# Normalisation factors applied behind the input projections of a four-layer hybrid block

## The reference, cut to what matters

```
def hybrid_layer(x, norm_g, w_in, w_out, ...):              # first kind, twice
    h = rmsnorm(x, norm_g)                                  # x * rsqrt(mean(x*x)+1e-6) * g
    proj = einsum("bsd,de->bse", h, w_in)                   # 14 pieces of 256 columns
    y_a = silu(layernorm(conv31(a_u*sigmoid(a_v)) + b)) * silu(a_z)
    y_b = b_b * conv3(b_c * b_x) * silu(b_z)
    y_c = window_gqa(...) * silu(c_z)      # keys at most 128 positions away
    y_d = neighborhood_attn(...) * silu(d_z)
    return x + concat(y_a, y_b, y_c, y_d) @ w_out

x = rmsnorm(x, final_norm_g)                                # between the two kinds

for l in range(2):                                          # second kind
    h = rms_norm(x, g_mix[l]);  proj = h @ w_in[l]
    # pool mixer; causal attention with rms_norm(q_lat, g_q), rms_norm(c_kv, g_kv);
    # a linear recurrence; gates = sigmoid(gate_logit + b_gate)
    x = x + (gates[0]*y_pool + gates[1]*y_mla + gates[2]*y_lru) @ w_out[l]
    h = rms_norm(x, g_ffn[l])
    x = x + square(relu(h @ w_ff1[l])) @ w_ff2[l]
return rms_norm(x, g_final)
```

## Time and profile before

| | |
|---|---|
| median of 3 runs | 2291.18 us (2290.15 to 2292.41) |
| the profiled execution: its time, its span | 2291.51 us, 2289.3 us |
| PE busy | 2085.9 us, 91% |
| weight loads of PE busy | 1728.9 us, 76% |
| DVE busy | 1306.3 us, 57% |
| ACT busy | 756.3 us, 33% |
| POOL busy | 1067.6 us, 47% |
| mean granted clock of PE | 0.945 of full speed |

### The profile page before, as it was taken

How to read it: one execution, slowest core, us unless ns; L and a number is a source line. 1 busy time by engine, 2 the same in 40 slices (tenths; PEclk the granted TensorE clock), 3 DMA queues, 4 the chain that set the end, 5 groups by cost and what they waited for, 6 DMA issues and landing times.

```text
span 2289.3 us, 30906 instructions
## 1 busy us (share of the span) xinstructions
PE 2085.9 (91%) x9708; PEld 1728.9 (76%) x9708; DVE 1306.3 (57%) x2241; ACT 756.3 (33%) x1101; POOL 1067.6 (47%) x1301
## 2 busy tenths in 40 slices
PE   5988887998887899979999999978899899999997
PEld 4877666877665788868788888867787788888886
DVE  5377766378768655464545535465555445535445
ACT  3232332332332344443232232234444323232231
POOL 3333244334233343456656655634435465656653
PEclk9999898999897899989999999989989899999998
DMA  4111112212111121122222222211222222222221
GB/s 153 64 57 71 38 56 80 76 55 74 38 56 67 56 74 55 74 92 85 89 100 95 92 92 96 106 63 57 73 73 74 77 107 79 106 92 92 96 98 62
DMA packets 28052, 179.66 MB, mean 78 GB/s; under 512 B 4000, under 2 KB 4128, under 8 KB 7456
## 3 DMA queue, kind: packets, MB, share of 16 engines
q1 hardware_dynamic: 24192, 169.88, 20.7%
q10 hardware_dynamic: 3744, 8.34, 1.1%
HBM read 176.11 MB, written 2.10 MB: 78 GB/s over the span
## 4 chain that ended last, share of the span: by engine, by line
issue 48%; POOL 35%; PE 17%; DVE 0%; POOLq 0%; DVEq 0%; ACT 0%
POOL W_lo L422 35%; PE bank L436 16%; POOLq L417 0%; DVE X L1626 0%; PE bank L486 0%; PE bank L479 0%; POOLq L419 0%; POOL spare L413 0%; DVE TMP L1283 0%; DVE PR L1328 0%; DVE PRE L1325 0%; DVE X L1989 0%; DVE PR L1986 0%; DVEq L182 0%; POOLq L422 0%
## 5 line engine op out<-in xcount | busy, mean ns | idle before, releaser
L422 POOL TENSOR_TENSOR W_lo<-W_raw,W_hi 128x256 fp32r<-128x256 f32 x1280 | 1065.7, 868 | 1189.7 <-ACT W_hi L867 1189.6
L436 PE MATMUL bank<-H_hi,W_hi 128*128 128x512 f32 x1392 | 560.3, 402 | 20.2 <-POOL W_lo L422 17.4
L436 PE MATMUL bank<-H_lo,W_hi 128*128 128x512 f32 x1392 | 549.8, 395 | 0.0
L436 PE MATMUL bank<-H_hi,W_lo 128*128 128x512 f32 x1392 | 549.7, 395 | 0.0
L867 ACT ACTIVATE W_hi<-W_raw 128x2048 fp32r<-128x2048 f32 x161 | 307.4, 1910 | 395.3 <-PE bank L436 382.5
L436 PE MATMUL bank<-Y_hi,W_hi 128*128 128x512 f32 x836 | 338.3, 405 | 21.9 <-DVE Y_lo L1268 11.8
L436 PE MATMUL bank<-Y_lo,W_hi 128*128 128x512 f32 x836 | 335.5, 401 | 0.0
L436 PE MATMUL bank<-Y_hi,W_lo 128*128 128x512 f32 x836 | 335.1, 401 | 0.0
L436 PEld LDWEIGHTS bank<-H_hi,W_hi 128*128 128x128 f32 x1392 | 267.4, 192 | 82.3 <-issue 22.3
L436 PEld LDWEIGHTS bank<-H_hi,W_lo 128*128 128x128 f32 x1392 | 265.9, 191 | 57.6
L436 PEld LDWEIGHTS bank<-H_lo,W_hi 128*128 128x128 f32 x1392 | 267.1, 192 | 53.0
(11 more groups left out here) (265 smaller groups left out, 2753.2 us busy)
## 6 DMA issues: line engine op xcount, KB each, us to landing
W_raw<-in_stream SPq DMA_DIRECT2D x160, 1024.0 KB, 4.8
BT<-in_bias ACTq DMA_DIRECT2D x8, 448.0 KB, 3.6
X<-in_x ACTq DMA_DIRECT2D x4, 512.0 KB, 9.7
out<-X SPq DMA_DIRECT2D x8, 256.0 KB, 2.2
BT<-in_rope ACTq DMA_DIRECT2D x2, 512.0 KB, 3.5
MC<-in_causal ACTq DMA_DIRECT2D x2, 320.0 KB, 3.0
MS<-in_window ACTq DMA_DIRECT2D x1, 320.0 KB, 11.0
CS<-in_rope ACTq DMA_DIRECT2D x1, 256.0 KB, 2.5
```

The lines of the kernel that those rows point to most:

```text
L422: ins = nc.gpsimd.tensor_tensor(W[1][:, s, part], W_raw[:, s, part], W[0][:, s, part].bitcast(F32), ALU.subtract)
L436: mm = pe.matmul(out, lhs[a], rhs[b], start=(not begun and k == 0 and a == 0 and b == 0), stop=(not more and k == n - 1 and a == 1), skip_ ...
```

## The change

Three things change.

1. The factor of a token, r = 1/sqrt(mean(x²)+eps), is the same for all features, so (X·r·g)W = ((X·g)W)·r. H is now the split of X·g, not of the normalised value. ACT makes H_hi from X with the gain as scale, DVE makes H_lo in one instruction (`norm_lo`), both for tile k as soon as output tile k of the layer before is added to X. PE starts the next layer's first unit at once and computes the sums of squares between its tiles 5 and 6. The factor, spread over partitions, is copied to SBUF (RB1, RB2), and each chunk's result is multiplied with it on DVE. For the second kind's first layer the norm between the kinds is folded in as well: a second sum (ACCG), with the squared gains, gives both factors, and X itself is normalised later (`norm_between`).
2. Blocks of 128 keys that the mask leaves out altogether are no longer computed (`b1_reach`, `b2_reach`): in the window attention two or three blocks a row of queries, not three; in the causal attention 1, 2, 3, 4 blocks, not 2, 2, 4, 4.
3. The hardware loops over the two layers of each kind are written out (`for l in range(DEPTH)`); the inner loops stay. The sums of squares in the feed-forward part are left out but for the last round.

The core of the diff:

```
+        def norm_lo(b, l, k, gain):
+            dve.wait_ge(b.hi.sem, b.hi.at(l, f"n{k}"))
+            nc.vector.scalar_tensor_tensor(H[1][:, k, :], X[:, k, :], gain, H[0][:, k, :].bitcast(F32),
+                                           ALU.mult, ALU.subtract).then_inc(...)
-            norm_to_h(b1, l, "n", "n", PAR1[:, P1["norm_g"]:P1["norm_g"] + KT])
+            mean(b1, l, "n")
+            diagonals(b1, l, "n")
+            nc.vector.tensor_copy(RB1[:, :], NB[:, :]).then_inc(dve_step, own.step())
...
+            def scaled(name, out, bank_):
+                nc.vector.tensor_tensor(out, bank_[:, :], RB1[:, :], ALU.mult) \
+                    .then_inc(b1.free.sem, own.event(b1.free, l, name))
+            def rescaled(out):
+                dve.wait_ge(*own.last(0))
+                nc.vector.tensor_tensor(out, out, RB1[:, :], ALU.mult).then_inc(dve_step, own.step())
...
                 elif kind in ("bz", "az"):                      # DVE
-                    dve.wait_ge(b1.aux.sem, b1.aux.at(l, name))
-                    nc.vector.scalar_tensor_tensor(pre, TH, 1.0, bank_[:, :], ALU.add, ALU.mult) \
-                        .then_inc(b1.free.sem, own.event(b1.free, l, name))
+                    scaled(name, pre, bank_)
+                    dve.wait_ge(b1.aux.sem, b1.aux.at(l, name))
+                    nc.vector.scalar_tensor_tensor(pre, TH, 1.0, pre, ALU.add, ALU.mult)
...
                 elif kind in ("dz", "cz", "bz", "az"):          # ACT
-                    nc.scalar.activation(TH, bank_[:, :], ACT.Tanh, scale=0.5)
+                    act.wait_ge(b1.free.sem, b1.free.at(l, name))
+                    nc.scalar.activation(TH, of, ACT.Tanh, scale=0.5)
...
+            for mm in by_tiles(pe, 0, H, lambda kt: pe.wait_ge(b1.lo.sem, b1.lo.at(l, f"n{kt}")),
+                               {6: lambda: pe_sums(pe, b1, l, "n", (ACC1,))} if l else {}):
                 mm.then_inc(b1.done.sem, 1)
+            if not l:
+                pe_sums(pe, b1, l, "n", (ACC1,))
+            chunk("dk0")
+            pe_spread(pe, b1, l, "n")
...
+    def b1_reach(i):
+        return ((0, 4), (0, 4)) if i < STEPS else (((0, 2), (0, 3)), ((0, 3), (1, 3)))[i % 2]
+    def b2_reach(s):
+        return (((0, 1), (0, 2)), ((0, 3), (0, 4)))[s % 2]
...
+                    def gate(s):                                # DVE, heads of the second kind
+                        dve.wait_ge(b2.done.sem, b2.done.at(l, f"g{jj}{s}", "h", j))
+                        nc.vector.tensor_tensor(out, G[c][:, :], RB2[:, :], ALU.mult) \
+                            .then_inc(b2.free.sem, own.event(b2.free, l, f"g{jj}{s}", "h", j))
```

More of the change, by code:

```diff
@@ L60 @@
 NP2 = _n
+GAINS = {"b1": (0, KT), "b2": (2 * KT, 3 * KT), "between": 4 * KT, "last": 5 * KT}
 COUNTS = []
@@ L929, in begin, with values @@
                     prep(1, l, k, (b1.done, l, B1_CHUNKS[2 * k - 3]))
+            def values(name, col):
+                act.wait_ge(b1.done.sem, b1.done.at(l, "ck1" if name == "cv" else name))
+                for t in range(4):
+                    act.wait_ge(*own.last(1))
+                    ins = nc.scalar.activation(AV[0][:, t, col:col + P], G[col // P if name[0] == "d" else 1]
+                                               [:, t * P:(t + 1) * P], ACT.Copy, scale=NR[:, t:t + 1])
+                    if t == 3:
+                        ins.then_inc(b1.hi.sem, own.event(b1.hi, l, name))
+                    else:
+                        ins.then_inc(act_step, own.step())
             def chunk(name, begun=False):
@@ L1644, in _ @@
+            diagonals(b2, l, "n", spread=False)
+            if not l:
+                dve.wait_ge(*own.last(1))
+                nc.vector.reciprocal(NR[:, 4:8], NR[:, 4:8]).then_inc(dve_step, own.step())
+                diagonal(bf, 0, "between", TMP[:, 1, :], 4)
             dve.wait_ge(par_in, 32 * l + 96)
             dve.wait_ge(*own.last(1))
-            nc.vector.tensor_scalar(HB[:, 0:4], PAR2[:, P2["b_a"]:P2["b_a"] + 4], 0.5, None, ALU.mult) \
+            nc.vector.tensor_scalar(HB[:, 0:28], HB[:, 0:28], 0.5, None, ALU.mult) \
@@ L1663, in _ @@
             mark(b2.acc, l, "kv")
+            dve.wait_ge(b2.bc.sem, b2.bc.at(l, "n"))
+            dve.wait_ge(*own.last(1))
+            nc.vector.tensor_copy(RB2[:, :], OB[:, :]).then_inc(dve_step, own.step())
             lam = PAR2[:, P2["lam"]:P2["lam"] + 2]
@@ L1712, in q_latent @@
                     mark(b2.acc, l, "q")
-            dve.wait_ge(b2.ss.sem, b2.ss.at(l, "kv"))
+            mean(b2, l, "kv", 2 * P, EPA[:, :])
             q_latent(0)
-            diagonals(b2, l, "kv")
+            diagonals(b2, l, "kv", spread=False)
+            if not l:
+                dve.wait_ge(bf.bc.sem, bf.bc.at(0, "between"))
+                norm_between(range(4))
+            dve.wait_ge(b2.bc.sem, b2.bc.at(l, "kv"))
             for k in (3, 4):
@@ L1723, in _ @@
             q_latent(1)
+            if not l:
+                norm_between(range(4, KT))
             q_latent(2)
@@ L2003, in _ @@
             own.leave(3)
[L2004 to L2009 removed]
+            down("f3", 0, True)
+        mean(bf, 0, "n")
+        diagonals(bf, 0, "n")
+        final_norm()
 def tables():
```

590 lines of the change are left out of this document (351 added, 239 removed).

## The result

The changed kernel took 2303.26 us in the median of four runs (2302.4 to 2305.71); the kernel before, run beside it, took 2290.66 us. The ratio is 1.0055 with a 95% interval of 1.0039 to 1.0071: it is slower by half a per cent. The forecast was 2264.7, in a range up to 2280, with a chance of 0.05 for slower.

A forecast was written before the change was run, and what follows sets the result against it. PE was taken to bound the whole, with DVE bounding the second kind's starts and the first kind's attention stage. Border gains less added DVE work summed to −26.8 us, from 2291.5 to 2264.7 us; range 2249 to 2280.

The forecast's parts named there:

- Rival 2: At the borders W_lo takes the norm's place: two units per border, 1 us each, some 6 us, so 2271; 15%.
- Rival 3: Attention stage, first kind: thirteen instructions and six DVE-ACT hand-overs cost 25.8 us a layer, so 2296, slower; 5%.
- start up to dk0, with the spread: Program start: dk0 begins at 37.0 not 43.48 us; less 1.05 for the spread between dk0 and dk1, −5.4.
- border in the first kind, with the spread: First kind, layer 1 to 2: PE's gap from o31 to dk0 shrinks from 31.4 to 13.0 us; with spread −17.4.
- first to second kind: Border between the kinds: PE's gap from o31 to q00 shrinks from 37.2 to 15.0 us, −22.1.
- starts of the second kind, both: DVE bounds these starts; later LS, the kr multiplication, the mean and norm_between add 8.2 us in the first layer, 5.0 in the second.
- first scores to first output unit, both layers: First kind's attention stage: DVE's additions in line, less shorter key-block rows, plus POOL contention: +10.2 us a layer, +20.4 in all.
- causal heads, both layers: Left-out key blocks save transposes and score products, 0.74 us per head pair, −5.9 over eight; gate multiplications cost nothing.
- middle and end of the second kind: Third gate's tanh waits for a DVE multiplication, 0.95 us a layer, +1.9; last norm's mean on DVE, +0.3.
- the trips: First kind's attention: DVE to ACT to DVE hand-overs in cz, bz and az, 7.7 us a layer.
- the multiplications behind au, bx and bb: First kind's attention: six a layer on DVE, only bx0, bb0 and bb1 in line, 2.2 us a layer.
- The term for LS: Starts of the second kind: DVE's little chain LS stands behind the copy of RB2, so begins 3.9 us later.

The follow-up runs named there:

- e1_early: The changed kernel with ACT rounding the values' W_hi ahead of AQ_hi of dq0, not behind AQ_hi of dq1; 2243.33 us, ratio 0.9785.
- e5_ls: As e1_early, with the chain LS ahead of the copy of RB2 on DVE in the second kind's start; 2241.06 us, ratio 0.9782.
- e9_best: e1_early with LS moved up, step 8's maxima between cz0's multiplication and gate, and W_hi ahead of H_hi in output units and last feed-forward round; 2234.88 us.
- e3_late8: The kernel before the change, with only the values' W_hi made once dk1 is projected, not once dq1 is; 2349.28 us, ratio 1.0249.

## Why the prediction was wrong, point by point

The step that failed is the sentence in the paragraph on the attention stage of the first kind: "From the projections' end to 137.80 PE has no pause, and DVE is busy 37.70 of 94.30, so the dq, dk, dv and dz multiplications cost nothing; that cover would be gone only with 50 us more of DVE." I measured the cover by DVE's busy time. What mattered was what stood behind the readers of dq in the list of another engine. A chunk's AQ_hi on ACT now waits for the factor, and the W_hi of the unit after next waits behind AQ_hi, while PE reaches that unit 7.8 us earlier than before. The sum moved dk0 forward and took for granted that the weights would follow. The runs showed in place of "cost nothing" a pause of 7.3 us and 19.7 us of low clock in each layer, 54 us in all. Before, AQ_hi read the bank, H had the factor in it already, and dk0 (at 390.82 in the earlier trace rows) was followed by the values without a pause. I listed the multiplication of dq and its cost, yet did not name what was queued behind the instruction that waits for it. Rival 2 had the right mechanism (W_lo takes the norm's place) but placed it at the by-tiles unit, at 1 us each, and without the clock; "the prepared units are two ahead" was wrong in just this place. Rival 3, the one on the slower side, named another mechanism and was not it.

Both parts are in the trace, and e1_early undid both: the pause, and the low clock in the values (41.2 us for 21.5). They are 54 of the 60 us that e1_early gave back; the rest lies in the first 5 us behind the values, which still had the low clock, and in the spread of the executions.

The other terms of the sum, the changed kernel against the profile before:

| term | forecast | measured |
|---|---|---|
| start up to dk0, with the spread | −5.4 | −7.8 |
| border in the first kind, with the spread | −17.4 | −17.7 |
| first to second kind | −22.1 | −22.3 |
| border in the second kind | −11.8 | −12.6 |
| starts of the second kind, both | +13.2 | +6.0 |
| first scores to first output unit, both layers | +20.4 | +17.8 |
| causal heads, both layers | −5.9 | −11.3 |
| output units of the first kind | 0 | +4.7 |
| middle and end of the second kind | +2.2 | about 0 |
| dk1 to the first scores, both layers | 0 | +53.9 |

Without the last row the sum is −43, and e1_early measured −48.6 with its own medians (2243.33 against 2291.98). So the chance of 0.92 for faster stood on terms that were mostly right or too cautious, and on one that was missing. The other terms didn't add up to the forecast either: they had −26.8 and measured −43, and e1_early, which has no missing term, is 21 us below the 2264.7 and below the 2249 of the range. The sum would have missed on that side too.

- The borders were right to within 1 us. The by-tiles unit took the 10.9 us at full clock that the earlier trace rows gave. The start of the program was 2.4 us better than forecast, and its arithmetic was wrong as well: 4.5 tiles at 3.4 us from 13.0 on and the rest at 2.2 end at about 36, not 34. The last H_lo was there at 32.3.
- The attention stage came near its forecast in part by luck. Without the low clock at its start it is +14.3 in e1_early and +12.8 in e5_ls, which has the same code there, against the 20.4. Within it the trips were forecast at 7.7 a layer and measured 6.6, the multiplications behind au, bx and bb were forecast at 2.2 and measured 3.4 to 5. What offset the second isn't settled.
- The row of 0.69 us at 706.32 in the earlier trace rows, compared there with 1.11 beside POOL, stands where POOL is idle. The same addition at 701.35, beside W_lo, took 0.69 us as well, so the comparison holds.
- The starts of the second kind cost less than half of the forecast. The term for LS was mis-sized: 3.9 a layer were forecast for it, and in the second layer the whole start grew by 1.7. How much of that is LS isn't shown, since e5_ls won only 1 us a layer by moving the chain, part of which the slower instructions took back.
- The heads gained twice the forecast. I had counted transposes and score products; the rest was not measured by itself and is open.
- The output units were costed at nothing. In the second layer PE waited 2.4 us for W_lo, since ACT's W_hi stands behind an H_hi that waits for DVE's addition; with W_hi ahead of it e9_best has 52.2 us there, and the changed kernel 54.8.

## What to carry to other kernels

When a change makes an instruction wait for something new, or brings one engine forward, read the list of the other engines from that place on and ask of each instruction who waits for it, and by when; the busy time of the engines doesn't show that. Ahead of a long run of narrow products a pause is worth removing even where it is short: 2.4 us of it cost 19 us more here, nearly as much again as the run takes at full clock. Where the pause couldn't be removed, 16 products of 512 columns in front of the run saved more than they cost. The change as a whole is good: with the order on ACT mended it is worth 2.1%, and with three more moves 2.5%.

## What the runs showed of the hardware

- What a pause costs in clock depended on the work behind it, and PE's busy time doesn't show it. Behind a pause of 7.3 us (7.7 in e3_late8) products of 128 columns stayed at the lower level (clock 0.50, 1.2 GHz) for all of 41.2 us, with PE and its weight loads busy all the time; without the pause the same products took 21.5 us at the upper one (2.4 GHz). With 16 products of 512 columns between the pause and them, at 0.57 in the mean, they ran at 1.00.
- The clock also fell behind a pause, not only in it. After 2.38 us of pause it fell 0.6 us into the values (40.7 us for them, at 0.51); after 0.64 us it fell 2.7 us into them in one layer and held in the other layer of the same execution. Its four executions are up to 21 us apart.
- A DVE instruction of 128x2 took 0.65 us beside POOL's W_lo and 0.16 without it, so a chain of small ones that moves into POOL's time grows too.
